# A one-core decoder step: the expert stage reordered, and the up projections made in split products

## The chip, the cores and the metric

The kernel runs on one core of a Trainium2 chip. The metric is the device time of one execution in microseconds (us); lower is better. Three runs of the kernel before gave 3391.62, 3391.7 and 3400.47 us, the median is 3391.7 us.

Engines are named as in the profile: PE multiplies matrices, PEld is its weight load, DVE is the vector engine, ACT the scalar engine, POOL GpSimd, SP the engine that only issues transfers. PSUM has eight banks, into which PE writes.

## What is computed

One layer is applied to T = 264 tokens: 256 of a prompt and 8 of a sample group. D is 2048.

```
proj  = rmsnorm(x) @ w_in                       # projections, attention, gated DeltaNet
x    += (sig(gA) * (o_fox @ w_up_fox) + sig(gB) * (o_gdn @ w_up_gdn)) @ w_out
h     = rmsnorm(x);  q = h @ w_q                # 8 heads, 2 x 128 keys each
s     = q . sub_keys;  two top-16 lists per head -> top-16 of 256 sums
idx, gate = ia * 128 + ib, softmax(top-16)      # 128 experts for each token
act   = gelu(h . u[idx]);  x += sum(act * gate * v[idx])     # 16384 experts
x    += sig(rmsnorm(x) @ w_ple_gate) * (p @ w_ple)
```

The kernel computes the expert part densely: for all 16384 experts it forms h . u, multiplies gelu of it by a weight that is zero where a token did not choose the expert, and multiplies by v.

## The kernel before

**Units.** All large weights pass through the core in units of 128 x 2048 f32 (1 MB), in the order of the list `STREAM`. SP loads a unit into one of four ring slots (`WR`). ACT copies each quarter of 512 columns to fp32r, the high part (`high_part`, L388); DVE subtracts it from the original to get the low part (`low_part`, L393). PE then makes three products for each 128 x 128 tile, high x high, high x low and low x high (`products`, L551 to L553): 48 matmuls of 264 columns for a unit. There is one buffer for the high and low parts of a quarter, so ACT may write a quarter only when PE is done with the same quarter of the unit before, and PE needs it three quarters later. Each engine follows an order written out by hand; `dense_steps` gives the usual one: four parts of the next unit, then the finishing work of this one.

**Up and out.** The two up projections (16 units) are plain f32 matmuls (L915) that read the ring slot directly. For each unit DVE multiplies the two results by their gates and adds (L1736 to L1740), ACT and DVE split the merged block into the parts that the out projection reads (L1200, L1742). `mt_ready` then releases the out projection (16 units, split products).

**Routing.** After the query projection `wq` PE multiplies queries and keys (`key_scores`, L942 and L934), and DVE finds the top-16 lists in three rounds, two of 128 tokens and one of the 8 sample tokens (`top16` and what follows, L1788 to L1851). `turn_results` turns each round's indices and gates over on PE.

**Gate weights, then experts, in two halves.** For 64 of the 128 first indices at a time, DVE makes one-hot rows (L1865, L1868), POOL multiplies them by the gates (L1335), PE multiplies the one-hots (L978) and ACT stores the dense gate weights of that half (L1231). Then come 128 units in groups: four units of u (scores, gelu L1249, weighing L1896 to L1900) and four of v (`outputs`, added to x by DVE at L1910). The loop body holds 16 units.

**After it** come the last norm and the per-layer embedding (16 units).

Of the kernel before, what the change touches and what calls it, by code (L numbers as in the profile page):

```python
# [15 lines left out]
ALU = mybir.AluOpType  # L16
# [23 lines left out]
HALF = N_KEYS // 2  # L40
PGW = NH * P
EG = 4

# [3 lines left out]
STREAM = [("A", 56), ("gates", 32), ("up", 16), ("out", 16), ("wq", 16), ("peer0", 128), ("peer1", 128), ("ple", 16)]  # L47
S0 = {}
_n = 0
for _name, _c in STREAM:  # L50
# [10 lines left out]
            ("norm1", 1), ("wq", 16), ("route", 12)]  # L61
for _h in range(2):
    JOB_LIST += [(f"wb{_h}", 66), (f"u{_h}", 64)]
JOB_LIST += [("norm2", 1), ("ple", 16)]
JOB = {}
SPLIT_JOBS = ("A", "gates0", "gates1", "out", "wq", "u0", "u1", "ple")
# [10 lines left out]
def split_index(s):  # L77

    return s if s < S0["up"] else s - 16


def stream_of(n):

    for name, s in (("A", S0["A"]), ("gates0", S0["gates"]), ("gates1", S0["gates"] + 16), ("out", S0["out"]),
                    ("wq", S0["wq"]), ("ple", S0["ple"])):
# [3 lines left out]
    for h in range(2):  # L89
        k = n - JOB[f"u{h}"]  # L90
        if 0 <= k < 64:
            return S0[f"peer{h}"] + (k if k < 4 else 4 + 8 * ((k - 4) // 4) + k % 4)
    return None
# [3 lines left out]
RS_JOBS = [[JOB["route"] + o for o in js] for js in ((0, 1, 2, 3), (4, 5, 6, 7), (9,))]  # L97
IDX_JOB = [JOB["route"] + o for o in (8, 10, 11)]
# [41 lines left out]
def build(nc, xT, pT, wd, vd, wsmall, wple, subk, kx, vx, lx, state, convst, params, consts, ptab,  # L140
          o_x, o_k, o_v, o_lf, o_sp, o_ss, o_cs):
    with ExitStack() as ctx:
# [37 lines left out]
        AL = AH + 2 * EG * T  # L180
        WSH, WSL = AH, AH + 384
        assert AL + 2 * EG * T <= NR
        sp_ = lambda a, n: split[:, a:a + n]
        as_f32 = lambda ap: ap.bitcast(F32)
        hh3 = sp_(HH, KT * T).rearrange("p (k t) -> p k t", t=T)
# [46 lines left out]
        WH = BIG  # L232
        AB = WH + HALF * T
        IDX = AB + 2 * T
        assert IDX + 3 * T <= BIG_END, IDX + 3 * T
        OHA = WR + 2 * D_MODEL
        OHB = OHA + 2 * 8 * HALF
        assert OHB + 2 * 8 * P <= WR + RING * D_MODEL

# [17 lines left out]
        assert SK >= HRAW + KT * T and SK + 16 * P <= IDX  # L257
        QZ = IDX + 3 * T
        assert QZ + 64 + NH * 136 <= BIG_END
# [33 lines left out]
        merged, mh_ready = sem("merged"), sem("mh_ready")  # L293
        ws_hi, ws_lo = sem("ws_hi"), sem("ws_lo")
        x_again = sem("x_again")
        aw_ready, ah_ready = sem("aw_ready"), sem("ah_ready")
# [36 lines left out]
        mg_step, oh_step = sem("merge_step"), sem("onehot_step")  # L333
# [16 lines left out]
        def bank(n):  # L350
            return ps[:, n % 4, :]

# [21 lines left out]
        def wait_slot(eng, it, m, s, back=0):  # L374

            if S0["up"] <= s < S0["out"]:
                eng.wait_ge(pe_job, it * m + (PJ[JOB["up"] + s - S0["up"]] - back))
            else:
                eng.wait_ge(lo_ready, it * (4 * m) + 4 * (split_index(s) + 1 - back))
# [49 lines left out]
        def _(sp):  # L429
# [70 lines left out]
            sp.wait_ge(mt_ready, 1)  # L500
# [3 lines left out]
            for half in range(2):  # L504
                s0, u0, v0 = S0[f"peer{half}"], 136 + 64 * half, 64 * half
                peel(s0, u0, PJ[JOB[f"wb{half}"] + 65])

                def group(it):

                    for kind in range(2):  # L510
                        for j in range(RING):
                            s = s0 + 4 + 4 * kind + j
                            wait_slot(sp, it, 8, s, RING)
                            load_w(it, 4, s, (wd, vd)[kind], ((u0 + 4) + j, v0 + j)[kind])

                with sp.Fori(0, 15) as it:
                    group(it)
                for j in range(RING):
                    wait_slot(sp, 0, 0, s0 + 120 + j)
                    load_w(0, 0, s0 + 124 + j, vd, v0 + 60 + j)  # L520
# [13 lines left out]
        def _(pe):  # L534
# [20 lines left out]
            def split_unit(it, m, s, n, mj=4, h0=None):  # L555


                if n >= 4 or not isinstance(it, int):
                    pe.wait_ge(evac[n % 4], it * (mj // 4) + n // 4)
                for q in range(RING):  # L560
                    wait_low_part(pe, it, m, s, q)
                    for kk in range(QK):
                        k = q * QK + kk
                        if h0 is not None:
                            pe.wait_ge(ht_ready, h0 + k + 1)
                        last = products(bank(n)[:, 0:T], ckh(q)[:, kk * P:(kk + 1) * P], ckl(q)[:, kk * P:(kk + 1) * P],
                                        hh3[:, k, :], hl3[:, k, :], k == 0, k == KT - 1)
                    last.then_inc(quarter_done, 1)

            def dense(name, its, h0=None):  # L570
                with pe.Fori(0, its) as it:
                    for j in range(RING):
                        split_unit(it, 4, S0[name] + j, JOB[name] + j, h0=None if j else h0)
# [333 lines left out]
            pe.wait_ge(of_ready, 1)  # L907
            with pe.Fori(0, 4) as it:
                for j in range(RING):
                    n = JOB["up"] + j  # L910
                    pe.wait_ge(w_loaded[j], it * 16 + 16 * (S0["up"] // 4 + 1))
                    pe.wait_ge(evac[n % 4], it + n // 4)
                    for half in range(2):
                        for k in range(NH):
                            last = mm(ps[:, n % 4 + 4 * half, 0:T], wr(j)[:, (half * NH + k) * P:(half * NH + k + 1) * P],  # L915
                                      ot3[:, half * NH + k, :], start=(k == 0), stop=(k == NH - 1))
                    last.then_inc(pe_job, 1)
            pe.wait_ge(mt_ready, 1)
            dense("out", 4)
# [6 lines left out]
            def key_scores(c):  # L926
                if c == 2:
                    n, = RS_JOBS[2]
                    claim(pe, n)
                    pe.wait_ge(qz_ready, 2)  # L930
                    for p_ in range(2):
                        for h in range(NH):
                            hp = 2 * h + p_
                            last = mm(bank(n)[0:64, p_ * P:(p_ + 1) * P], at(QZ + hp * 64, 64), at(SK + hp * P, P),  # L934
                                      start=(h == 0), stop=(h == NH - 1))
                    last.then_inc(pe_job, 1)
                    return
                for g, n in enumerate(RS_JOBS[c]):
                    claim(pe, n)
                    for i in range(4):  # L940
                        hp = 4 * g + i
                        last = mm(bank(n)[:, i * P:(i + 1) * P], at(QT + hp * T + c * P, P), at(SK + hp * P, P),  # L942
                                  start=True, stop=True)
                    last.then_inc(pe_job, 1)

            def turn_results(c):
                n = IDX_JOB[c]
                claim(pe, n)
                pe.wait_ge(res_ready, c + 1)
                for i in range(3):  # L950
                    if c == 2:
                        last = mm(bank(n)[:, i * P:i * P + NS], at(LX + i * P, P, 64), at(ROW_T, NS, 64), start=True, stop=True)
                    else:
                        last = nc.tensor.transpose(bank(n)[:, i * P:(i + 1) * P], at(RES + i * P, P), ident)  # L954
                last.then_inc(pe_job, 1)

            key_scores(0)
            key_scores(1)
            turn_results(0)
            key_scores(2)  # L960
            turn_results(1)
            turn_results(2)


            for half in range(2):
                wb, ub = JOB[f"wb{half}"], JOB[f"u{half}"]

                def weights_of(it, j):


                    pe.wait_ge(oha_ready, it * 4 + (33 * half + j + 1))
                    pe.wait_ge(ohb_ready, it * 4 + (33 * half + j + 1))
                    for n in (wb + 2 * j, wb + 2 * j + 1):
                        pe.wait_ge(evac[n % 4], it * 2 + n // 4)
                        for i in range(4):
                            t = 4 * (n - wb - 2 * j) + i
                            oha = at(OHA + (j % 2) * 8 * HALF + t * HALF, HALF)
                            last = mm(bank(n)[:, i * P:(i + 1) * P].rearrange("p (r a) -> p r a", a=HALF),  # L978
                                      at(OHB + (j % 2) * 8 * P + t * P, P),
                                      oha.unsqueeze(1).broadcast_to([P, 2, HALF]), start=True, stop=True)  # L980
                        last.then_inc(pe_job, 1)

                with pe.Fori(0, 8) as it:
                    for j in range(4):
                        weights_of(it, j)
                weights_of(8, 0)

                s0 = S0[f"peer{half}"]

                def scores(it, m, s, n):  # L990
                    for j in range(RING):
                        split_unit(it, m, s + j, n + j, m // 2)

                def outputs(it, m, s, g, buf):

                    for dq in range(RING):
                        for q in range(RING):
                            if dq == 0 and q == 0:
                                pe.wait_ge(a_blk, it * (m // 2) + (4 * (16 * half + g) + 4))

                            pe.wait_ge(y_added, it * (2 * m) + (16 * (16 * half + g) + 4 * dq + q + 1))
                            wait_low_part(pe, it, m, s + dq, q)
# [1023 lines left out]
```

## Time and profile before

| | us |
|---|---|
| median of three runs | 3391.7 |
| profiled execution, first to last instruction (its span) | 3393.9 |
| PE busy in it | 3112.1 |
| DVE busy | 1973.4 |
| ACT busy | 1291.3 |
| POOL busy | 190.1 |

The profile is one execution. Its span is the only time that it gives of itself. It lies 2.2 us above the median and within the three runs. PE's busy time counts overlapping matmuls once; groups of matmuls on different lines overlap each other, so their sums exceed the span.

### The profile page before, as it was taken

To read this page: it belongs to the slowest core of one execution; us is meant where nothing else is said; L and a number is where in the kernel's file an instruction comes from. 1 tells how busy PE (TensorE), PEld (TensorE's weight loads), DVE (VectorE), ACT (ScalarE), POOL (GpSimd) and SP (SyncE) were. 2 spreads that over 40 slices of the span, in tenths; PEclk is the share of its full clock that TensorE was granted. 3 is DMA by queue.
4 is the path that set the end of the run, shared out by engine and by line. 5 is a ranking of instruction groups with operands and counts; after the bars stand their busy time and mean duration, and the time that the engine had idled before them with its cause. 6 is when DMAs were issued, how large, how long until landed. Compare 5 with 4: busy or idle time off the path is not lost.

```text
span 3393.9 us, 63208 instructions
## 1 busy us (share of the span) xinstructions
PE 3112.1 (92%) x23603; PEld 2921.9 (86%) x23603; DVE 1973.4 (58%) x3888; ACT 1291.3 (38%) x2225; POOL 190.1 (6%) x203
## 2 busy tenths in 40 slices
PE   6999899799999998922899999999889999999989
PEld 6999689499755787922799999999889999999979
DVE  4477466422233235488766666666766666666654
ACT  4455320122222024411544444444444444444444
POOL 0000110000000000002400000000330000000000
PEclk8999899599999999966999999999999999999989
DMA  5555200356576444400155455455225554545543
GB/s 192 177 184 180 85 1 8 127 199 245 200 250 214 185 160 148 173 0 0 70 180 184 177 182 182 177 185 175 73 99 176 184 179 180 184 175 185 178 148 125
DMA packets 82022, 519.76 MB, mean 153 GB/s; under 512 B 9186, under 2 KB 9458, under 8 KB 28914
## 3 DMA queue, kind: packets, MB, share of 16 engines
q1 hardware_dynamic: 69394, 468.36, 38.8%
q0 software_dynamic: 11360, 45.61, 3.7%
q10 hardware_dynamic: 1152, 4.19, 0.3%
q8 instruction: 78, 1.28, 0.1%
q14 instruction: 38, 0.31, 0.0%
HBM read 508.74 MB, written 9.39 MB: 153 GB/s over the span
## 4 chain that ended last, share of the span: by engine, by line
PE 88%; DVE 7%; POOL 2%; SPq 2%; issue 1%; ACT 0%; DMA 0%; POOLq 0%; DVEq 0%; ACTq 0%
PE ps L551 23%; PE ps L552 23%; PE ps L553 22%; PE ps L915 3%; PE ps L858 3%; PE ps L869 3%; PE ps L978 2%; POOL arena L1335 2%; PE ps L732 1%; SPq L465 1%; PE ps L611 1%; DVE arena L1865 1%; PE ps L546 1%; PE ps L720 1%; PE ps L603 1%
## 5 line engine op out<-in xcount | busy, mean ns | idle before, releaser
L551 PE MATMUL ps<-split 128*128 128x264 f32 x6288 | 1798.0, 286 | 53.9 <-DVE split L393 53.9
L552 PE MATMUL ps<-split 128*128 128x264 f32 x6288 | 1789.7, 285 | 0.0
L553 PE MATMUL ps<-split 128*128 128x264 f32 x6288 | 1784.7, 284 | 0.0
L393 DVE TENSOR_TENSOR split<-arena,split 128x512 fp32r<-128x512 f32 x1568 | 1078.6, 691 | 956.9 <-ACT split L388 954.1
L388 ACT ACTIVATE split<-arena 128x512 fp32r<-128x512 f32 x1568 | 987.8, 632 | 1401.5 <-PE ps L553 1401.1
L551 PEld LDWEIGHTS ps<-split 128*128 128x128 f32 x6288 | 1187.9, 189 | 73.9 <-issue 36.2
L552 PEld LDWEIGHTS ps<-split 128*128 128x128 f32 x6288 | 1188.3, 189 | 0.8
L553 PEld LDWEIGHTS ps<-split 128*128 128x128 f32 x6288 | 1183.6, 188 | 0.3
L1910 DVE TENSOR_TENSOR arena<-arena,ps 128x264 f32<-128x264 f32 x512 | 216.4, 423 | 5.9 <-PE ps L553 5.9
L1335 POOL TENSOR_TENSOR arena<-arena 128x512 f32<-128x512 f32 x66 | 121.7, 1844 | 1264.6 <-DVE arena L1865 1264.6
L978 PE MATMUL ps<-arena 128*128 128x128 f32 x1056 | 140.3, 287 | 38.9 <-POOL arena L1335 38.8
L978 PEld LDWEIGHTS ps<-arena 128*128 128x128 f32 x1056 | 128.3, 197 | 50.9 <-POOL arena L1335 32.9
L1231 ACT ACTIVATE arena<-ps 128x256 f32 x132 | 84.3, 638 | 106.7 <-PE ps L978 106.7
L915 PE MATMUL ps<-arena 128*128 128x264 f32 x512 | 116.8, 390 | 0.7 <-DVE arena L1721 0.7
L858 PE MATMUL ps<-arena 128*64 128x128 f32 x1024 | 116.0, 272 | 0.0
L915 PEld LDWEIGHTS ps<-arena 128*128 128x128 f32 x512 | 98.4, 192 | 18.8 <-issue 0.8
L858 PEld LDWEIGHTS ps<-arena 128*64 128x64 f32 x1024 | 112.2, 136 | 2.3
L869 PE MATMUL ps<-arena 128*8 128x512 f32 x256 | 112.7, 592 | 0.0
L954 PE MATMUL ps<-arena 128*128 128x128 f32 x6 | 1.8, 434 | 101.8 <-ACT arena L1216 51.8
L869 PEld LDWEIGHTS ps<-arena 128*8 128x8 f32 x256 | 21.5, 89 | 78.6 <-issue 76.0
L954 PEld LDWEIGHTS ps<-arena 128*128 128x128 f32 x6 | 1.0, 213 | 102.2 <-ACT arena L1216 52.0
L1865 DVE TENSOR_TENSOR arena<-arena 128x512 f32<-128x512 f32 x66 | 57.7, 875 | 40.1 <-PE ps L978 40.1
(299 smaller groups left out, 1696.4 us busy)
## 6 DMA issues: line engine op xcount, KB each, us to landing
arena<-in_wd SPq DMA_DIRECT2D x280, 1024.0 KB, 4.8
arena<-in_vd SPq DMA_DIRECT2D x128, 1024.0 KB, 4.8
arena<-in_kx POOLq DMA_DIRECT2D x32, 512.0 KB, 6.4
arena<-in_kx SPq DMA_DIRECT2D x32, 512.0 KB, 4.5
arena<-in_vx SPq DMA_DIRECT2D x32, 512.0 KB, 4.3
arena<-in_vx POOLq DMA_DIRECT2D x32, 512.0 KB, 4.4
arena<-in_state POOLq DMA_DIRECT2D x8, 512.0 KB, 6.7
o_ss<-arena ACTq DMA_DIRECT2D x8, 512.0 KB, 7.5
```

The source lines that it names most:

```text
L388: nc.scalar.activation(ckh(q), at(WR + (s % 4) * D_MODEL + q * QW, QW), ACT.Copy).then_inc(hi_ready, 1)
L393: nc.vector.tensor_tensor(ckl(q), at(WR + (s % 4) * D_MODEL + q * QW, QW), as_f32(ckh(q)), ALU.subtract).then_inc(lo_ready, 1)
L551: mm(out, wh, xh, start=start, stop=False)
L552: mm(out, wh, xl, start=False, stop=False)
L553: return mm(out, wl, xh, start=False, stop=stop)
L858: last = mm(score[:, j, :], at(QM + (s * NH + h) * 64, 64), page(j)[:, h * P:(h + 1) * P], start=False, stop=False, skip_group_check=True)
L869: last = mm(ps[0:NS, b + i, :], at(PRT + j * 64 + s * NH, NH), page(j)[:, i * 512:(i + 1) * 512], start=(j == 0), stop=(j == PAGES - 1))
L915: last = mm(ps[:, n % 4 + 4 * half, 0:T], wr(j)[:, (half * NH + k) * P:(half * NH + k + 1) * P], ot3[:, half * NH + k, :], start=(k == 0), ...
L978: last = mm(bank(n)[:, i * P:(i + 1) * P].rearrange("p (r a) -> p r a", a=HALF), at(OHB + (j % 2) * 8 * P + t * P, P), oha.unsqueeze(1).br ...
L1335: nc.gpsimd.tensor_tensor(oh, oh, gate, ALU.mult).then_inc(oha_ready, 1)
L1865: V.tensor_tensor(oh, cst(C_IOTA + half * HALF, HALF).unsqueeze(1).broadcast_to([P, 8, HALF]), ia, ALU.is_equal).then_inc(oh_step, 1)
L1910: V.tensor_tensor(xt3[:, d, :], xt3[:, d, :], ps[:, 4 + q, 0:T], ALU.add).then_inc(y_added, 1)
```

## The change

**Order of the expert stage.** All 128 units of u come first, written out unit by unit on every engine, then all 128 units of v, in a loop whose body holds 8 units. One buffer of gelu results is no longer enough, so the scores of each pair of units are written to device memory (`scores_spill`) and read back by POOL, four units at a time.

**Routing beside the scores.** Only the first `key_scores` stands before the units. The second comes after unit 2, the turned results after units 19, 36 and 41. On DVE the operations of the top-16 lists and the low parts of the u units are woven together: `beside` counts estimated time of routing work and puts in one low part for every 0.8 us of it; `lows_until` forces the low parts up to a unit before DVE waits for PE or ACT. The expected places of ACT's exponentials and of the turned results are constants (`EXP_AT`, `TURN_AT`).

**Gate weights beside the scores.** They are built for 4 tokens a step, 66 steps, all 128 first indices at once. 33 steps follow units 43 to 64 and 33 follow units 95 to 116, one or two for a unit. The first half of the tokens is written to device memory (`gates_spill`) after units 67 to 89, the second half stays on chip.

**Weighing.** POOL multiplies scores by gate weights, eight operations of 132 columns for a group of four blocks. ACT makes the high part and DVE the low part, beside the v units.

**Up projections.** They become split units like the others: ACT and DVE split `ot` (the branch outputs) into the operand parts and each up unit into high and low parts. The merged blocks keep their place in the gates' buffer; ACT makes their high parts beside the up units, DVE the 16 low parts after the last merge, and the first out unit waits for these one by one (`ml_ready`).

```diff
-STREAM = [("A", 56), ("gates", 32), ("up", 16), ("out", 16), ("wq", 16), ("peer0", 128), ("peer1", 128), ("ple", 16)]
+STREAM = [("A", 56), ("gates", 32), ("up", 16), ("out", 16), ("wq", 16), ("u", 128), ("v", 128), ("ple", 16)]
+EXP_AT = (13, 30, 38)
+TURN_AT = (19, 36, 41)
+W_FROM = (43, 95)
+SPILL_AT = tuple(67 + 3 * i // 2 for i in range(N_KEYS // SPILL))
...
# PE, up and scores
-            pe.wait_ge(of_ready, 1)
+            pe.wait_ge(ol_ready, 5)
...
+                    for q in range(RING):
+                        wait_low_part(pe, it, 4, S0["up"] + j, q)
+                        for i in range(QK):
+                            k = q * QK + i
+                            last = products(ps[:, n % 4 + 4 * (k // NH), 0:T], ckh(q)[:, i * P:(i + 1) * P],
+                                            ckl(q)[:, i * P:(i + 1) * P], hh3[:, k, :], hl3[:, k, :], k % NH == 0, k % NH == NH - 1)
+                        last.then_inc(quarter_done, 1)
...
+            for k in range(N_KEYS):
+                split_unit(0, 4, S0["u"] + k, JOB["u"] + k)
+                if k == KEYS1:
+                    key_scores(1)
+                for c in range(3):
+                    if k == TURN_AT[c]:
+                        turn_results(c)
+                if k == TURN_AT[0]:
+                    key_scores(2)
+                for g in w_steps_after(k):
+                    build_weights(g)
...
+            with pe.Fori(0, GROUPS // 2) as it:
+                for b in range(2):
+                    outputs(it, 2 * EG, S0["v"] + EG * b, b)
...
# SP
+            for k in range(N_KEYS):
+                wait_slot(sp, 0, 0, S0["u"] + k - RING)
+                load_w(0, 0, S0["u"] + k, wd, 136 + k)
+                if k >= 6 and k % 2 == 0:
+                    write_scores(k - 6)
...
# ACT, in each u unit
+                if k >= 4 and k % 2 == 0:
+                    act.wait_ge(g_saved[(k // 2) % 2], 16 * (k // 4))
+                n = JOB["u"] + k
+                A(at(GST + (k % 4) * T, T), bank(n)[:, 0:T], ACT.Gelu).then_inc(evac[n % 4], 1)
...
# POOL
+            for g in range(GROUPS):
+                pool.wait_ge(gw_in[g % 2], 32 * (g // 2 + 1))
+                for j in range(EG):
+                    nc.gpsimd.tensor_tensor(score(g, j)[:, 0:TH], score(g, j)[:, 0:TH], weight(g, j), ALU.mult).then_inc(am_ready, 1)
+                    nc.gpsimd.tensor_tensor(score(g, j)[:, TH:T], score(g, j)[:, TH:T], kept(g, j), ALU.mult).then_inc(am_ready, 1)
+                if g == 0:
+                    for b in range(2):
+                        pool.wait_ge(g_saved[b], 16 * (N_KEYS // 4))
+                if g:
+                    pool.wait_ge(a_blk, EG * g)
+                if g + 1 < GROUPS:
+                    load_group(g + 1)
...
# DVE
+            def beside(us):
+
+                spent[0] += us
+                while spent[0] >= 0.8:
+                    spent[0] -= 0.8
+                    lows_until(lows[0] + 1)
...
+            def make_rows(g):
+
+                if g >= 2:
+                    dve.wait_ge(route_pe, ROUTE_JOBS + g - 1)
+                V.tensor_tensor(at(OHB + (g % 2) * WT * P, WT * P).rearrange("p (t b) -> p t b", b=P),
+                                cst(C_IOTA).unsqueeze(1).broadcast_to([P, WT, P]),
+                                at(IDX + T + WT * g, WT).unsqueeze(2).broadcast_to([P, WT, P]), ALU.is_equal).then_inc(ohb_made, 1)
+                for t in range(WT):
+                    n = WT * g + t
+                    ins = V.tensor_scalar(gate_rows(g, t), cst(C_IOTA), at(IDX + n, 1), at(IDX + 2 * T + n, 1), ALU.is_equal, ALU.mult)
+                ins.then_inc(rows_made, 1)
+
+            def rest_weighed(it, m, g, j):
+
+                dve.wait_ge(ah_ready, it * m + (EG * g + j + 1))
+                V.tensor_tensor(a_low(g, j), score(g, j), as_f32(a_high(g, j)), ALU.subtract).then_inc(a_blk, 1)
...
+            def add_outputs(it, m, s, g, last=False):
+
+                for dq in range(RING):
+                    for q in range(RING):
+                        if not (last and dq == RING - 1):
+                            low_part(dve, it, m, s + dq + 1, q)
+                        wait_quarter(dve, it, m, s + dq, q)
+                        d = 4 * dq + q
+                        V.tensor_tensor(xt3[:, d, :], xt3[:, d, :], ps[:, 4 + q, 0:T], ALU.add).then_inc(y_added, 1)
+                    if not last:
+                        rest_weighed(it, m, g + 1, dq)
```

## Rows read from the trace of the kernel before

**Rows 1.** Windows: start:end, length, busy PE, PEld, DVE, ACT, POOL, clock, DMA.
```profile
1453.95:1582.76 128.81, 15.21 (x109) 14.04 (x108) 117.85 (x509) 7.34 (x14) 0.00 (x0) 0.57 0.00 0
1582.76:1673.33 90.57, 70.19 (x528) 64.20 (x528) 66.29 (x66) 42.68 (x68) 61.29 (x33) 0.95 0.01 2
1673.33:2418.97 745.64, 744.76 (x6144) 744.58 (x6144) 507.06 (x959) 341.57 (x576) 0.00 (x0) 1.00 0.51 180
2418.97:2509.75 90.78, 70.15 (x528) 64.07 (x528) 66.53 (x67) 42.69 (x68) 60.38 (x33) 0.96 0.01 1
...
1119.72:1236.56 116.84, 116.81 (x512) 98.37 (x512) 24.55 (x60) 6.34 (x15) 0.48 (x1) 0.98 0.42 153
1236.56:1334.73 98.17, 94.58 (x768) 94.37 (x768) 50.74 (x83) 40.53 (x65) 0.00 (x0) 0.98 0.54 193
```

**Rows 2.** What PE waited for in 1673 to 3255: total, times, longest.
```profile
PE ps L978 <- POOL arena L1335: 19.4, 31, 3.2
PE ps L551 <- DVE split L393: 4.1, 2, 2.1
```

**Rows 3.** Chain that ended last, in order of time: start, length, work.
```profile
703.23 7.18 PE ps L858 x64
716.41 7.18 PE ps L858 x64
...
1595.13 2.07 PE ps L978 x16
```

**Rows 4.** Groups by line and shape: busy, mean ns, idle before.
```profile
L942 PE MATMUL ps<-arena 128*128 128x128 f32 x64 | 7.4, 275 | 0.5 <-issue 0.5
...
L1822 DVE TENSOR_TENSOR arena<-arena 128x2048 f32<-128x2048 f32 x4 | 9.0, 2284 | 0.0
...
L1305 POOL TENSOR_SCALAR arena<-arena 128x128 f32<-128x128 f32 x16 | 5.7, 371 | 20.8 <-PE ps L675 14.8 <-PE ps L690 6.0
```

**Rows 5.** Windows over the first two rounds of lists, columns as in rows 1.
```profile
1459.06:1513.00 53.94, 2.80 (x26) 2.61 (x24) 53.28 (x229) 1.49 (x3) 0.00 (x0) 0.56 0.00 0
1515.18:1569.00 53.82, 3.99 (x30) 3.75 (x29) 53.26 (x229) 0.31 (x1) 0.00 (x0) 0.56 0.00 0
```

**Rows 6.** Timeline of DVE in the v units: start, length, operation, idle before.
```profile
3237.02 0.69 DVE L393 TENSOR_TENSOR split<-arena,split 128x512 fp32r<-128x512 f32 x1 [0.43 <-ACT split L388]
3237.63 0.42 DVE L1910 TENSOR_TENSOR arena<-arena,ps 128x264 f32<-128x264 f32 x1
```

**Rows 7.** Timeline from the last up unit to the first out unit.
```profile
1238.62 2.19 ACT L388 ACTIVATE split<-arena 128x512 fp32r<-128x512 f32 x4
...
1239.36 2.50 DVE L393 TENSOR_TENSOR split<-arena,split 128x512 fp32r<-128x512 f32 x4 [0.21 <-ACT split L388]
...
1240.11 0.59 PE L551 MATMUL ps<-split 128*128 128x264 f32 x1 [3.58 <-DVE split L393]
```

**Rows 8.** Timeline from the last page of v to the first up unit.
```profile
1107.72 7.05 PE L869 MATMUL ps<-arena 128*8 128x512 f32 x16
...
1114.80 1.21 DVE L1712 TENSOR_TENSOR arena<-ps,arena 8x1024 f32<-8x1024 f32 x1 [18.59 <-PE ps L869]
...
1119.72 3.88 PE L915 MATMUL ps<-arena 128*128 128x264 f32 x8 [0.67 <-DVE arena L1721]
```

**Rows 9.** DMA issues: transfer, queue, count, size, median us to landing.
```profile
o_ss<-arena ACTq DMA_DIRECT2D x8, 512.0 KB, 7.5
...
arena<-in_kx POOLq DMA_DIRECT2D x32, 512.0 KB, 6.4
```

**Rows 10.** Timeline of DVE beside POOL where the gate weights are built.
```profile
1583.37 1.22 DVE L1868 TENSOR_TENSOR arena<-arena 128x1024 f32<-128x1024 f32 x1
1583.67 1.82 POOL L1335 TENSOR_TENSOR arena<-arena 128x512 f32<-128x512 f32 x1 [463.47 <-DVE arena L1865]
1584.50 1.53 DVE L1865 TENSOR_TENSOR arena<-arena 128x512 f32<-128x512 f32 x1
...
1589.44 0.69 DVE L1865 TENSOR_TENSOR arena<-arena 128x512 f32<-128x512 f32 x1 [2.27 <-PE ps L978]
```

More of the change, by code:

```diff
@@ L910, in _ @@
                     n = JOB["up"] + j
-                    pe.wait_ge(w_loaded[j], it * 16 + 16 * (S0["up"] // 4 + 1))
                     pe.wait_ge(evac[n % 4], it + n // 4)
[L913 to L919, printed above, removed]
+                    for q in range(RING):
[5 more added lines that the diff above has]
+                        last.then_inc(quarter_done, 1)
+            dense("out", 4, xh3=mh3, rest=ml_ready)
             norm(1)
@@ L959, in _ @@
[L959 to L1002, printed above, removed]
-                            for j in range(EG):
-                                a = (buf * EG + j) * T
-                                last = products(ps[:, 4 + q, 0:T], ckh(q)[:, j * P:(j + 1) * P],
-                                                ckl(q)[:, j * P:(j + 1) * P], sp_(AH + a, T), sp_(AL + a, T),
-                                                j == 0, j == EG - 1)
-                            last.then_inc(quarter_done, 1)
-                scores(0, 0, s0, ub)
-                with pe.Fori(0, 7) as i2:
-                    for b in range(2):
-                        scores(i2, 16, s0 + 4 + 8 * b, ub + 4 + 4 * b)
-                        outputs(i2, 16, s0 + 8 + 8 * b, b, b)
-                scores(0, 0, s0 + 116, ub + 60)
-                outputs(0, 0, s0 + 120, 14, 0)
-                outputs(0, 0, s0 + 124, 15, 1)
@@ new lines, in _, with merged_high @@
+            for q in range(RING):
+                high_part(act, 0, 0, S0["up"], q)
+            act.wait_ge(of_ready, 1)
+            act.wait_ge(oh_ready, 4)
+            A(hh3[:, 0:NH, SEQ:T], ot3[:, 0:NH, SEQ:T], ACT.Copy).then_inc(oh_ready, 1)
+            def merged_high(it, j):
+                act.wait_ge(merged, it * 4 + (j + 1))
+                m = arena[:, bass.ds(it * (4 * T) + (GT + j * T), T)]
+                A(split[:, bass.ds(it * (4 * T) + (MH + j * T), T)], m, ACT.Copy).then_inc(mh_ready, 1)
@@ new lines, in values @@
+            def values(it, m, s, g, last=False):
+                for j in range(EG):
+                    for q in range(RING):
+                        if not (last and j == EG - 1):
+                            high_part(act, it, m, s + j + 1, q)
+                    if not last:
+                        split_weighed(it, m, g + 1, j)
+            with act.Fori(0, GROUPS // 2 - 1) as it:
+                for b in range(2):
+                    values(it, 2 * EG, S0["v"] + EG * b, b)
+            values(0, 0, S0["v"] + EG * (GROUPS - 2), GROUPS - 2)
@@ L1747, in add_to_x @@
+            dense_steps(dve, S0["up"], 4, low_part, merge, False, False)
+            for k in range(KT):
+                if k == 0:
+                    dve.wait_ge(mh_ready, KT - 1)
+                if k == KT - 1:
+                    dve.wait_ge(mh_ready, KT)
+                V.tensor_tensor(hl3[:, k, :], blk(GT, k), as_f32(mh3[:, k, :]), ALU.subtract).then_inc(ml_ready, 1)
             def add_to_x(it, j):
@@ L1754, in _ @@
             dve.wait_ge(x_again, 16)
-            dense_steps(dve, S0["out"], 4, low_part, add_to_x)
+            dense_steps(dve, S0["out"], 4, low_part, add_to_x, first=False)
             for j in range(RING):
@@ L1923, in _ @@
+            with dve.Fori(0, GROUPS // 2 - 1) as it:
+                for b in range(2):
+                    add_outputs(it, 2 * EG, S0["v"] + EG * b, b)
+            add_outputs(0, 0, S0["v"] + EG * (GROUPS - 2), GROUPS - 2)
+            add_outputs(0, 0, S0["v"] + EG * (GROUPS - 1), GROUPS - 1, True)
+            dve.wait_ge(y_added, 4 + GROUPS * KT)
             dve.sem_inc(x2_ready, 1)
```

448 lines of the change are left out of this document (236 added, 212 removed).

## The prediction, made before the changed kernel ran

> **What bounds the kernel now.** I read the stage windows first [rows 1]. In the unit stages PE is the bound: in the first half of the expert stage it is busy for 744.8 of 745.6 us at the full clock of 2.4 GHz (1.00), while DVE works 507 and ACT 342. That is 745.6 / 128 = 5.83 us for a unit, 1.46 us for a quarter. PE's waits inside the two halves come to 4.1 us on the low parts of the weights [rows 2]. So nothing but fewer matmuls shortens a unit, and a unit is free for other engines as long as the low parts come in time. What remains are the stretches in which PE waits. The reader is to see three: routing takes 128.8 us with PE busy for 15.2 and DVE for 117.9, at a clock of 0.57, and the gate weights take 90.6 and 90.8 us with no unit running. The other place is the up stage, 116.8 us, where PE is busy but on plain f32 passes.
>
> **The expert stage: what is removed.** The three stretches vanish from PE's path: 128.8 + 90.6 + 90.8 = 310.2 us. What comes back, on PE unless said:
>
> Key scores and turned results are the same matmuls, so PE's busy time of the routing window returns, 15.2 us, with the 0.5 us wait ahead of it [rows 1, 4]: 15.7.
>
> Gate weights: 66 steps of 4 matmuls, each two passes in f32, 528 passes; before it was 1056, since each half handled all tokens. A pass costs 0.112 us with 64 weight columns (7.18 / 64) and 0.129 in the old weights (2.07 / 16) [rows 3]; the same shape in the key scores costs 7.4 / 64 = 0.115 [rows 4]. I take 0.115: 60.7 us (59.1 to 68.1).
>
> Changing over from unit to other matmuls and back: in the gate stage, whose units are also written out one by one, one unit with 64 page passes takes 716.41 - 703.23 = 13.18 us [rows 3]. Less 7.18 and 5.83, that leaves 0.17. There are 44 units with weight steps and four with routing work: 48 x 0.17 = 8.2 us (0 if it is hidden, 11.9 at one for each of 70 insertions). This row also answers for the unrolled code: 17 instructions a us were issued there without a gap, as many as a unit now needs (96 in 5.83 us).
>
> Routing on DVE costs nothing where it fits between low parts. A low part holds DVE for 0.61 us (3237.02 to 3237.63 [rows 6]), four for a unit are 2.4 of 5.83. The estimates in `beside` sum to 46.3 us for a full round (lists 18.0 + 12.9, sums 2.6, selection 11.8, 1.0), so 57 low parts are woven in, 14.25 units. DVE then needs 53.9 [rows 5] + 57 x 0.61 = 88.7 us, PE 14.25 x 5.83 + 3.7 for the second key scores = 86.8. The second round: 53.8 + 58 x 0.61 = 89.2 against 84.5 + some 5.6 of turned results and third key scores. The two are level. A low part may be late by three quarters less ACT's copy and its own time, 4.37 - 0.6 - 0.7 = 3 us, before PE notices. Single selection operations of 2.28 us [rows 4] use up most of that slack, several times. I take 3 us of stalls; ends: 0, and 11 if low parts occupy their full 0.69. After unit 43 DVE has the one-hot rows instead, one and a half steps a unit at 0.69 for 512 columns [rows 10] and four of 128 columns at 0.25, an estimate between a quarter of that and its half: 5.0 with the low parts, in units that PE then makes 5.83 + 1.5 x 0.92 long. Covered; if it were not, each us over would be paid 44 times.
>
> The waits. ACT's exponentials and PE's turned results stand in their queues behind units whose low parts DVE has already been forced to issue (`lows_until`), so what the high parts queue behind is ready. Gelu of a unit waits for a score write issued some 16 us earlier (the ring has four blocks); the longest landing of a write row is 7.5 us [rows 9]. SP's score writes stand ahead of weight loads, but their gelu is done when the slot before them comes free. All this I cost at nothing. If the writes took 1 us more than the ring allows, every second unit would pay it, 64 us.
>
> u to v: the first v quarter needs the last score weighed, which stands on DVE behind the fourth low part of v. High part and low part of the last quarter (1.3 us), the subtraction 0.43: PE stops for 2.0 us (1 to 3.6, the stop before the out stage [rows 7]). Group 1 then needs the buffer of the last scores: gelu and write (3 to 7 us), POOL's load (6.4 [rows 9]), a multiplication, its high part, a low part behind it: 13 to 18 us after the last u unit. PE wants it at 2.0 + 2 x 5.83 = 13.7. I take 1.5 us, once (0 to 5). Later groups have 23.3 us for a load and eight multiplications.
>
> The v loop has the products, low parts and additions of before. Sum: 15.7 + 60.7 + 8.2 + 3 + 2 + 1.5 = 91.1 back, so the stage gains 219.1.
>
> **POOL beside DVE** is the one cost that the trace makes me weigh. Where the gate weights were built, DVE's L1865 takes 0.69 us alone, but 1.53 when it starts beside POOL's multiplication: POOL ends at 1585.49, DVE at 1586.03 [rows 10]. It stood still until POOL was done. POOL's 1.82 in turn begins under DVE's L1868, which ends at 1584.59; 0.90 remain for 512 columns. The new multiplications have 132 columns; bounds are 0.37 for 128 columns with one tile read [rows 4] and 1.82 [rows 10]. I take 0.4, nearest in size. Eight are 3.2 us of standing still for a group. DVE's idle in 16 quarters is 16 x 0.43 [rows 6] = 6.9 us, less four new subtractions of 0.35 (0.42 for 264 columns, less the 0.08 by which operations overlap): 5.5. Hidden. The Trainium skill, "SBUF — State Buffer", section "Who interferes with whom", states it as a lock: a DVE instruction with two SBUF inputs and a GpSimd instruction that reads SBUF exclude each other for the whole instruction. The trace agrees (1.53 against 0.69 us). By it the low parts wait and the additions, which read PSUM, do not; by the rows alone, with 3.2 against 5.5, the sum is the same.
>
> **Up and out.** Removed 116.8. The units now cost 16 x 5.83 = 93.2. Their start is late: after the last gate unit (1107.7) ACT makes four copies of 1024 columns, 1.1 each by its 2.19 for four of 512 [rows 7], and DVE four subtractions of some 1.2 and four low parts (2.5), in order, before L1712. That ends about 1116.5, where L1712 began at 1114.80 [rows 8]: 1.7 late, and 0.7 for the split of the last columns. The clock of 0.98 in 116.8 us [rows 1] means 4.7 us at 1.2 GHz, which costs 2.3; it stays. The stop before the out stage was 3.58 us [rows 7]; now it is high and low part (1.4), three merge steps (1.2), one low part and a signal (0.7): 3.3. The other 15 low parts take 0.35 each, PE's three products 0.364 (5.83 / 16). Sum: -116.8 + 93.2 + 1.7 + 0.7 + 2.3 - 0.3 = -19.2 (-23 to -15).
>
> **Together**: 3393.9 - 219.1 - 19.2 = 3155.6 for the span. The median lay 2.2 us under the span, so 3153.
>
> **The rivals.**
>
> *DVE sets the pace of units 0 to 42.* For: 88.7 against 86.8, before any waiting. Against: 3 us of slack, and the rounds end with low parts alone. If each of 172 low parts cost PE 0.15 us: 26 us in place of the 3, 3176.
>
> *POOL's lock outgrows DVE's idle time in the v loop.* At 0.9 us a multiplication it is 7.2 - 5.5 = 1.7 us a group, 32 groups: 54 us, 3207. For: L1865's 1.53. Against: the sum above. The rule that makes it possible is the one named above (the Trainium skill, "SBUF — State Buffer", section "Who interferes with whom").
>
> *The same, slower than before.* At 1.82 us it is 14.6 - 5.5 = 9.1 a group: 291 us, 3444. It decides at 5.5 + 238 / 32 = 12.9 us a group, 1.6 us a multiplication. For: the row's 1.82. Against: half of that was waiting, for four times the columns.
>
> *Routing isn't hidden.* If the waits in the weave left PE standing while DVE works the lists, up to 117.9 us come back: 3271. Against: DVE's list work waits for PE nowhere but at the turned results.
>
> **How the numbers follow.** Forecast 0.66, its own range 3137 (no change-over, no stalls) to 3183 (upper ends of the passes, of DVE and of both hand-overs together). DVE's pace 0.13, POOL's lock at 0.9 0.09, slower 0.03, routing exposed 0.05; 0.04 for what I don't see, half of it near no change. The range is 3137 to 3200: it takes in DVE's pace and leaves out the rest. A change under 0.3% (10 us) can't be told from none. Faster 0.95, same 0.02, slower 0.03.
>
> **What would show it.** PE without stops of over 10 us from the last query unit to the last v unit; 5.83 us a unit in both halves, 7.3 in units 43 to 64 and 95 to 116; up near 96 us; POOL's multiplications at 0.4 us and low parts beside them at 0.7 to 1.1. I am wrong if PE's waits on L393's successor exceed 20 us, if a v group takes over 23.5 us, or if ACT waits for score writes.

## The result and the profile after

The changed kernel took 3272.5 us in the median (3272.3 to 3278.6) against 3393.2 for the kernel before on the same chip: a ratio of 0.9639, 95% interval 0.9622 to 0.9656. It is faster, but by 121 us where 238 were forecast (219.1 + 19.2); 3272 lies far above the range of 3137 to 3200. The profiled span is 3277.0 us (before 3393.9). One execution of the last experiment took 7611.3 us where its other three took 3142.7 to 3148.9; it is left out of every comparison.

The 116.9 us between the two spans lie as follows, to 0.1 us, by the starts in the chains of the two traces. Up and out gain 22.7 (216.9 to 194.2 us) and lose 2.0 by a later start; the stretch from the second norm to the key scores loses 1.6, the stages ahead of up lose 4.7, in which nothing was changed. The expert stage gains 102.6 (1802.0 to 1699.4), where 219.1 were forecast. Of the miss, 116.5 us lie in that stage. Its windows answer to [rows 1] (columns as there): three of the u units, one of the v loop, and, last, the up stage.

```profile
1443.99:1716.00 272.01, 266.60 (x2176) 264.39 (x2176) 228.67 (x690) 133.81 (x233) 0.00 (x0) 0.99 0.55 190
1716.00:1875.00 159.00, 159.00 (x1339) 159.00 (x1338) 111.98 (x248) 97.26 (x145) 0.00 (x0) 1.00 0.47 161
...
2047.00:2260.00 213.00, 213.00 (x1787) 213.00 (x1786) 139.02 (x289) 124.58 (x195) 5.88 (x10) 1.00 0.52 181
2300.00:2600.00 300.00, 274.70 (x2106) 272.45 (x2105) 200.20 (x395) 124.59 (x220) 68.66 (x110) 0.94 0.51 184
...
1126.46:1223.00 96.54, 94.66 (x768) 94.45 (x768) 59.95 (x111) 43.68 (x79) 0.00 (x0) 0.98 0.51 186
```

The u units are what the prediction wanted: PE stands for 5.4 of 272 us while routing runs beside the units, and not at all from 1716 to 2260. The v loop, which was thought to be untouched, is not: in 300 us PE stands for 25 and its clock is 0.94. It makes 2106 matmuls there; at the pace of [rows 1] (6144 in 745.64) it would make 2472. What PE waits for, answering to [rows 2]:

```profile
PE ps L606 <- DVE split L1985: 73.5, 32, 2.4
PE ps L606 <- DVE split L441: 51.6, 10, 15.6
...
PE ps L606 <- DVE split L1821: 3.1, 1, 3.1
```

The second row lies almost all in earlier stages (5.3 us of it in the u units), the third is the stop before the out stage (3.3 forecast). The first is new: 32 stops, one for each group of v, for L1985. That is the subtraction in `rest_weighed`. The timeline shows why, first three rows of POOL and DVE for later use, then the end of group 1 (columns as in [rows 6]):

```profile
2290.61 0.92 POOL L1395 TENSOR_TENSOR arena<-arena 128x132 f32<-128x132 f32 x1
...
2291.49 0.47 POOL L1396 TENSOR_TENSOR arena<-arena 128x132 f32<-128x132 f32 x1
...
2291.68 0.82 DVE L441 TENSOR_TENSOR split<-arena,split 128x512 fp32r<-128x512 f32 x1
...
2318.64 0.63 ACT L436 ACTIVATE split<-arena 128x512 fp32r<-128x512 f32 x1 [0.83 <-PE ps L608]
2319.17 0.41 ACT L1279 ACTIVATE split<-arena 128x264 fp32r<-128x264 f32 x1
2319.30 0.69 DVE L441 TENSOR_TENSOR split<-arena,split 128x512 fp32r<-128x512 f32 x1 [0.43 <-ACT split L436]
2319.91 0.42 DVE L2004 TENSOR_TENSOR arena<-arena,ps 128x264 f32<-128x264 f32 x1
...
2320.25 0.43 DVE L1985 TENSOR_TENSOR split<-arena,split 128x264 fp32r<-128x264 f32 x1
...
2320.90 0.39 PE L606 MATMUL ps<-split 128*128 128x264 f32 x1 [2.30 <-DVE split L1985]
2321.13 0.30 PE L607 MATMUL ps<-split 128*128 128x264 f32 x1
2321.25 0.40 PE L608 MATMUL ps<-split 128*128 128x264 f32 x1
```

PE finishes the group's last quarter at 2318.60. That frees the place for the last high part on ACT (2318.64), and behind it stand, in program order, DVE's low part of it (2319.30), the addition of the quarter just finished (L2004), and only then the subtraction of the next group's fourth score block (L1985). PE's first quarter of the next group waits for that one (`a_blk`). ACT's copy of the block (L1279) was done at 2319.58, POOL's product long before. So two queues make up the stop of 2.3 us: ACT's high part and copy, which end 0.98 us after PE does, and DVE's low part and addition, which put the subtraction off until 2320.25.

The rest of the v loop's loss is the clock. Behind such a stop PE's passes follow each other at 0.22 us in place of 0.12 (2321.45 and 2321.67 are the next two starts). Over the v loop from 2284 to 3130 PE was busy for 774.4 us with 5942 matmuls; the run without these stops (below) has 5979 in 726.0, which makes 721.5 for 5942. So 53 us are clock and 71.6 are stops.

The chain in the u units, answering to [rows 3]: a gate-weight step has 8 passes, two steps in one unit and one in the next.

```profile
1717.65 1.78 PE ps L1022 x16
1725.23 0.89 PE ps L1022 x8
1731.92 1.78 PE ps L1022 x16
```

A pass costs 1.78 / 16 = 0.111 us. Two units with their 24 passes take 14.27 us: 2.67 for the passes, 5.80 for a unit. That is no more than the 5.83 of a unit in [rows 1], so these rows leave nothing for changing over between them.

### The profile page after: what moved, and what is told of

It reads as the page before. It is cut to its first block, busy times and chain, and to the rows that moved or that the text cites. A ratio compares the mean times of both kernels' runs of the same rounds, so it can differ in the third digit from the quotient of the medians.

```text
span 3277.0 us, 60857 instructions
## 1 busy us (share of the span) xinstructions
PE 3068.8 (94%) x23331; PEld 2899.6 (88%) x23331; DVE 1905.2 (58%) x3899; ACT 1363.1 (42%) x2361; POOL 269.7 (8%) x457
## 4 chain that ended last, share of the span: by engine, by line
PE 87%; DVE 7%; SPq 2%; issue 1%; ACT 1%; DMA 1%; POOL 0%; DVEq 0%; ACTq 0%; POOLq 0%
PE ps L606 24%; PE ps L607 24%; PE ps L608 23%; PE ps L916 4%; PE ps L927 3%; PE ps L1022 2%; DVE split L441 2%; PE ps L790 2%; SPq L513 1%; PE ps L669 1%; PE ps L601 1%; PE ps L778 1%; PE ps L661 1%; ACT split L436 1%; SPq L514 1%
## 5 line engine op out<-in xcount | busy, mean ns | idle before, releaser
L606 PE MATMUL ps<-split 128*128 128x264 f32 x6544 | 1903.2, 291 | 129.8 <-DVE split L1985 73.5
L607 PE MATMUL ps<-split 128*128 128x264 f32 x6544 | 1883.4, 288 | 0.0
L608 PE MATMUL ps<-split 128*128 128x264 f32 x6544 | 1876.7, 287 | 0.0
L441 DVE TENSOR_TENSOR split<-arena,split 128x512 fp32r<-128x512 f32 x1632 | 1134.3, 701 | 1062.1 <-ACT split L436 1051.5
L606 PEld LDWEIGHTS ps<-split 128*128 128x128 f32 x6544 | 1259.1, 192 | 157.9 <-DVE split L441 118.9
L607 PEld LDWEIGHTS ps<-split 128*128 128x128 f32 x6544 | 1260.6, 193 | 0.8
L608 PEld LDWEIGHTS ps<-split 128*128 128x128 f32 x6544 | 1253.9, 192 | 0.3
L2004 DVE TENSOR_TENSOR arena<-arena,ps 128x264 f32<-128x264 f32 x512 | 215.9, 422 | 3.0 <-PE ps L608 3.0
L1395 POOL TENSOR_TENSOR arena<-arena 128x132 f32<-128x132 f32 x128 | 89.1, 696 | 169.9 <-DMA arena<-gates_spill 169.9
L1396 POOL TENSOR_TENSOR arena<-arena 128x132 f32<-128x132 f32 x128 | 84.9, 663 | 0.0
L1979 DVE TENSOR_SCALAR arena<-arena 128x128 f32<-128x128 f32 x264 | 73.6, 344 | 0.0
L1274 ACT ACTIVATE arena<-ps 128x512 f32<-128x512 f32 x66 | 69.8, 1130 | 0.0
L1022 PE MATMUL ps<-arena 128*128 128x128 f32 x528 | 66.1, 274 | 0.0
L1022 PEld LDWEIGHTS ps<-arena 128*128 128x128 f32 x528 | 62.7, 191 | 0.0
L1102 ACT ACTIVATE arena<-ps 128x264 f32 (+1 forms) x120 | 45.0, 375 | 40.0 <-PE ps L608 39.9
L1985 DVE TENSOR_TENSOR split<-arena,split 128x264 fp32r<-128x264 f32 x128 | 54.7, 427 | 2.3 <-ACT split L1279 2.3
```

Source lines behind the costliest of these rows:

```text
L441: nc.vector.tensor_tensor(ckl(q), at(WR + (s % 4) * D_MODEL + q * QW, QW), as_f32(ckh(q)), ALU.subtract).then_inc(lo_ready, 1)
L606: mm(out, wh, xh, start=start, stop=False)
L607: mm(out, wh, xl, start=False, stop=False)
L608: return mm(out, wl, xh, start=False, stop=stop)
L1022: last = mm(bank2(n)[:, t * P:(t + 1) * P], at(OHB + ((g % 2) * WT + t) * P, P), gate_rows(g, t), start=True, stop=True)
L1395: nc.gpsimd.tensor_tensor(score(g, j)[:, 0:TH], score(g, j)[:, 0:TH], weight(g, j), ALU.mult).then_inc(am_ready, 1)
```

## The experiments

**The fourth block's weighing moved ahead.** In ACT's loop and in DVE's the fourth block is handled behind the second quarter of the group's last unit; the other three stay behind the fourth quarter of theirs.

```diff
-                    if not last:
-                        rest_weighed(it, m, g + 1, dq)
+                        if not last and q == (1 if dq == EG - 1 else RING - 1):
+                            rest_weighed(it, m, g + 1, dq)
```

> The changed kernel with one edit: in each v group, ACT's high part and DVE's subtraction for the last block of the next group stand behind the second quarter of the fourth unit, not behind its last. Theory (stop and clock): PE stops 2.3 us at the head of each of 32 groups, because the last subtraction stands behind the last addition, and runs at the lower clock after it; both go, 73.5 + some 53 us, so 3146 to 3155 us and a clock of 1.00 in the v units. Rival (POOL's lock): DVE is late because of POOL's multiplications and the stop only shows it; then at most a few us a group come back, above 3230. Rival (the clock falls by itself): only the stops go, 3199.

Measured: 3154.5 us (3146.9 to 3155.0), ratio 0.9272 [0.9249, 0.9295]: 118 us below the changed kernel, by one `if` on each engine. PE's waits for L1985 fall from 73.5 to 2.0 us, which is the one at the first v group. Its v loop:

```profile
2300.00:2600.00 300.00, 300.00 (x2471) 300.00 (x2470) 237.53 (x464) 146.18 (x257) 81.02 (x130) 1.00 0.61 215
```

PE stands nowhere, at the full clock, with POOL's multiplications and the low parts as before. So the place of the fourth block's weighing, at the end of ACT's and DVE's orders, is the cause of the miss. The edit moves both the copy and the subtraction; the next one parts them.

**A shorter stop.** Only DVE's subtraction moves, to just ahead of the group's last low part; ACT's copy stays where it was.

```diff
+                        if not last and dq == EG - 1 and q == RING - 1:
+                            rest_weighed(it, m, g + 1, dq)
                         if not (last and dq == RING - 1):
                             low_part(dve, it, m, s + dq + 1, q)
...
-                    if not last:
+                    if not last and dq < EG - 1:
```

> The changed kernel with one edit: only DVE's subtraction for the last block moves, ahead of the group's last low part and addition; ACT's high part of that block stays behind the last quarter. The stop should shrink from 2.3 to about 1.5 us and not vanish. Theory (stop and clock): if the clock still falls after a stop of 1.5 us, 3272 - 31 x 0.8 = 3247; if it no longer falls, 3195. Rival (POOL's lock): no change, 3272.

Measured: 3208.4 us (3204.4 to 3211.3), ratio 0.9435 [0.9413, 0.9457]. There are still 32 stops, of 1.7 us (54.0 in all). DVE now stands and waits for ACT's copy (a row from the end of a group), so the subtraction's place on DVE alone is not the whole cause. But the clock does not fall:

```profile
2288.74 0.43 DVE L1985 TENSOR_TENSOR split<-arena,split 128x264 fp32r<-128x264 f32 x1 [0.73 <-ACT split L1279]
...
2300.00:2600.00 300.00, 279.89 (x2280) 277.44 (x2279) 217.75 (x428) 135.01 (x238) 72.21 (x117) 1.00 0.55 199
```

Of the 54 us above the run before, 52 are the stops (54.0 less the 2.0 that stayed there). Against the changed kernel it gains 64 us, only 19.5 of them shorter stops.

**Between the two.** The subtraction behind the last low part, ahead of the last addition.

```diff
                             low_part(dve, it, m, s + dq + 1, q)
+                        if not last and dq == EG - 1 and q == RING - 1:
+                            rest_weighed(it, m, g + 1, dq)
                         wait_quarter(dve, it, m, s + dq, q)
```

> The changed kernel with DVE's subtraction of the next group's fourth block put behind the group's last low part but ahead of its last addition (in the changed kernel it is behind the addition). The stop loses the addition's 0.42 us: 2.3 - 0.4 = 1.9 us in 32 groups, PE waits about 60 us on it. If a stop of 1.9 us leaves the clock at 2.4 GHz as one of 1.7 us does, the time is 3154.5 + 60 = 3215; if the clock falls as it does behind stops of 2.3 us, some 45 us more: 3260.

Measured: 3257.2 us (3251.7 to 3260.1), ratio 0.9584 [0.9567, 0.9601]. PE waits 63.0 us in 32 stops, 2.0 us each, and the clock falls:

```profile
2300.00:2600.00 300.00, 278.34 (x2168) 276.09 (x2167) 209.31 (x407) 128.36 (x226) 73.49 (x118) 0.95 0.51 187
```

PE stands for 21.7 of 300 us here and for 20.1 in the run ahead of this one, nearly the same, but the matmuls fall from 2280 to 2168. In this loop stops of 1.7 us leave the clock at 2.4 GHz (1.00), stops of 2.0 don't (0.95). Of the 103 us above 3154.5, 61 are stops and some 42 are clock.

**POOL's work doubled.** Of the rivals that would take the time out of the range, the one with the highest chance (0.09) was that POOL's multiplications hold DVE up. The first experiment's kernel does each of them twice, the second time into unused space.

```diff
+                    for i, other in enumerate((weight(g, j), kept(g, j))):
+                        nc.gpsimd.tensor_tensor(cst(C_INV + (2 * j + i) * TH, TH), score(g, j)[:, i * TH:(i + 1) * TH], other, ALU.mult).then_inc(twice, 1)
```

> The kernel of the run with the last block early, and POOL does each of its multiplications a second time into unused space (the result isn't read): 16 of 132 columns for a group. Theory (stop and clock): POOL's multiplications are hidden in DVE's idle 5.5 us a group and partly wait themselves; the time stays within 10 us of the run with the last block early. Rival (POOL's lock): 16 x 0.68 us = 10.9 us of lock for a group against 5.5 us of idle, (10.9 - 5.5) x 32 = 172 us more, about 3320.

Measured: 3156.2 us (3148.0 to 3156.6), ratio 0.9276 [0.9253, 0.9300], no different from 3154.5.

```profile
2300.00:2600.00 300.00, 300.00 (x2472) 300.00 (x2471) 243.86 (x465) 146.18 (x259) 154.77 (x242) 1.00 0.61 215
```

POOL is busy for 155 us in place of 81, and PE still never stands. The lock itself is there: in the timeline above a low part of 0.69 us takes 0.82 beside POOL, and POOL's 0.47 becomes 0.92. But DVE's busy time grows by only 6.3 us in the 300 (237.5 to 243.9), and its idle time takes that. The rival is refuted.

**Fewer low parts beside routing.** DVE issues a low part for every 1.0 us of estimated list work instead of 0.8.

```diff
-                while spent[0] >= 0.8:
-                    spent[0] -= 0.8
+                while spent[0] >= 1.0:
+                    spent[0] -= 1.0
```

> The changed kernel with fewer low parts per unit of routing work on DVE: one for each 1.0 us of estimated list work in place of 0.8. If DVE and PE are level in units 0 to 42, as the prediction had it, a unit's four low parts now wait behind 4 x 0.2 = 0.8 us more of lists; over the 14 units of each of two weavings that is 11 us each: PE waits 15 to 25 us for low parts in the u stage, and the time is 3288 to 3298 in place of 3272. If DVE has slack that the trace of before did not show, PE's waits for low parts in the u stage stay under 8 us and the time stays within 4 us of 3272.

Measured: 3286.0 us (3282.5 to 3291.0), ratio 0.9669 [0.9652, 0.9686], 13.5 us above the changed kernel. PE's waits for low parts in the u units, the changed kernel's first and then this one's:

```profile
PE ps L606 <- DVE split L441: 5.3, 6, 3.0
```

```profile
PE ps L606 <- DVE split L441: 13.0, 19, 2.3
```

They grow by 7.7 us, and the first subtraction L1985 starts 13.1 us later (2.2 of which were there at the key scores already). The waits, 13.0 us in all, are less than the 15 to 25 expected of a DVE without slack and more than the 8 of one with plenty. I read it as DVE and PE nearly level in these units, with a little slack on DVE. At 0.8 the rival "DVE sets the pace" did not come about, but it was near.

**The up projection alone**, in the kernel before, whose expert stage stays as it was.

> The kernel before with the change to the up projection alone (split products, the merge in DVE's place between the low parts, merged columns split for the out stage); the expert stage is that of before. If the two parts of the change don't touch each other, the saving is the one read from the two profiles, up start to the end of out: 216.9 - 194.2 = 22.7 us, less 2.0 for the later start, some 20 us: 3372 against 3393, a ratio near 0.994. Rival: part of these 20 us came from the stages ahead of it (another clock at the hand-over from the gates); then under 12 us are left.

Measured: 3411.9 us (3408.9 to 3418.9) against 3395.0, ratio 1.0045 [1.0031, 1.0060]: slower by 17 us where 20 were to be gained. Up and out themselves do gain (194.3 us from the first up product to the norm, as in the changed kernel). The loss is in the second half of the expert stage, which the edit doesn't touch. Waits of PE, and a few of its pieces in the chain:

```profile
PE ps L551 <- issue: 15.8, 6, 2.7
...
PE ps L553 <- issue: 8.2, 6, 1.8
```

```profile
2614.10 1.08 issue
...
2619.25 1.57 issue
...
2713.16 1.30 issue
...
2719.22 0.59 issue
```

PE waits for nothing that the profile shows but its next instruction, twice in each of six turns of the loop of 16 units (99 us apart). In that half, 2500 to 3250, the instruction queue moved 64 packets; in the kernel before 13 (queue, packets, MB, share):

```profile
q8 instruction: 64, 1.05, 0.5%
```

```profile
q8 instruction: 13, 0.21, 0.1%
```

That is 51 packets more in some seven turns. I read it so: the loop's code, held over all its turns in the kernel before, is here fetched again in each. The price in that window (columns as in [rows 1]):

```profile
2500.00:3250.00 750.00, 725.98 (x5875) 723.19 (x5874) 484.86 (x916) 327.21 (x554) 0.00 (x0) 0.98 0.49 174
```

24 us of stops, and 13 of clock (5875 matmuls take 713 at the pace of [rows 1]): 37 lost. Is it the edit's doing, or only that the longer up stage ahead of the loop moved its code? Three kernels get 128 more PE instructions, waits for a semaphore reached long ago, where PE stands for the second norm anyway:

```diff
             norm(1)
+            for _ in range(128):
+                pe.wait_ge(ws_lo, 1)
```

The up projection alone, moved:

> The kernel of the run with the up projection alone, with 128 more PE instructions (waits for a semaphore that has long been reached) where PE waits for the second norm's sums anyway; nothing else differs. In that run the up stage gained what it should, but in the second half of the expert stage the instruction queue moved 64 packets in place of 13, and PE stopped for its next instruction twice in each turn of the unit loop. Theory: whether the loop's code stays on the chip hangs on where it lies in the program, and the more PE rows ahead of it moved it. Then 128 more can end the stops (some 3375, 13 packets in each half) or leave them, or bring them to the first half. Rival: the stops come from the up projection's other doings (weights, splits); then nothing changes: 3412, 64 packets in the second half and 13 in the first. A result without stops refutes the rival; one with the same stops tells little.

Measured: 3420.3 us, ratio 1.0061 [1.0044, 1.0077], no faster, but the stops have changed places. They now lie in the first half, with 64 packets there, and the second half has 11:

```profile
1780.45 1.33 issue
...
1785.65 1.75 issue
...
1879.73 1.29 issue
```

The kernel before, moved:

> The kernel before with the same 128 more PE instructions at the same place, and no other edit. If the place of the loop's code decides alone, a kernel that computes exactly what it did may now stop for its code in one of the halves: some 37 us longer for one half (what the run with the up projection alone lost in its second half), 3430. If the place does not matter: 3393 to 3397 and 13 packets in each half.

Measured: 3394.9 us, ratio 0.9994 [0.9983, 1.0005]; 13 packets in the second half, 12 in the first, no stops.

The first of them refutes that the new up stage's computing makes the stops: waits that compute nothing took them out of one half and put them into the other. So it matters where the loop's code lies. That this alone decides isn't shown, and which places are bad the runs don't tell: with the new up stage one of the two halves was hit each time, in the kernel before neither half at either place.

**All four weighings moved**: in each group to quarters of units 2 and 3 (and for group 0 to u units 120 to 123), so that the change from u to v has no stop either.

```diff
+WEIGH_AT = {(2, 0): 0, (2, 2): 1, (3, 0): 2, (3, 1): 3}
...
-                    if not last:
-                        rest_weighed(it, m, g + 1, dq)
+                        if not last and (dq, q) in WEIGH_AT:
+                            rest_weighed(it, m, g + 1, WEIGH_AT[dq, q])
```

> The changed kernel with all weighing for the next group in the third and fourth unit of a group, done by the second quarter of the fourth, and the first group weighed beside u units 120 to 123. Theory: the stops at the heads of the groups go as in the run with the last block early; the stop between u and v (2 us) and the wait for the scores of the second group (some 3 us), with the lower clock behind them, go too: 5 to 9 us below that run, about 3142. Rival: that wait is set by the write and load of the last scores and stays; then it equals the run with the last block early.

Measured: 3149.6 us (3139.8 to 3150.7), ratio 0.9255 [0.9231, 0.9280], 5 us below the first experiment, which is within the spread of the runs of either; but PE no longer waits for this subtraction anywhere, 2.0 us less. The same kernel with the 128 waits:

> The fastest version so far (the changed kernel with all four weighings of a group moved to quarters with slack) with the same 128 more PE instructions at the same place. Its unit code before the v loop is passed once, and its v loop has 8 units in place of 16. If half the loop's size is what keeps its code on the chip wherever it lies: 3150 within 5 us, under 12 packets on the instruction queue in the v loop, no stops for code. If a loop of 8 units can be moved out of place as one of 16 can: stops of 2 to 3 us in each of 16 turns, 40 us and more: 3190.

Measured: 3144.6 us, ratio 0.9245 [0.9227, 0.9264], 7 packets in 2510 to 3250 and no stops for code. In the two places tried, the loop of 8 units has no such stops.

## Why the prediction was wrong

The step that failed is "The v loop has the products, low parts and additions of before." The prediction did see the four new subtractions of a group, and costed them as time on DVE: four of 0.35 us against idle time, hidden. As time they are hidden: with the last one moved, PE stands nowhere, though all four are still there. But the weighing of the last block, ACT's copy and DVE's subtraction, was last in both queues at the moment when PE had nothing else, and its cost is not its length but the length of the queues ahead of it. The prediction had followed exactly this wait at one place, "u to v", and priced it right, at 2.0 us. It did not see that the same wait comes at the end of every group. 32 stops of 2.3 us are 73.5 us, and the fall of the clock behind them, which it had not considered there, is 53 more in the profile. Its own mark for being wrong, a v group of over 23.5 us, is met: the starts at 2293.41 and 2320.90 are 27.5 us apart.

The rival "Routing isn't hidden" gives 3271, within 2 us of the measured time. That is chance: PE stands for 5.4 us beside routing, not 117.9.

With that step mended by one edit the kernel takes 3154.5 against the forecast of 3153. That is closer than the terms were, and partly luck: the u units came out 9 us shorter than forecast, the stages ahead of the expert stage in which nothing was changed 6.3 us longer. The ends of the prediction's own range, 3137 and 3183, do not follow from the terms named for them, which give some 3142 and 3174. The terms:

- The three stretches gone from PE's path (310.2 us): right. No stop of over 3 us is left between the key scores and the last v unit.
- The u units: some 829 us forecast from 1443.99 on (745.6 for units, 60.7 + 8.2 + 3, and the 11.4 of 15.7 that lie behind the first key scores), measured 819.5 to PE's stop at 2263.5. Passes were 0.111 for 0.115 (2 us), changing over 0 for 8.2 us, stalls 5.3 for 3. The 0.17 us taken from the gate stage did not carry over; PE waits for nothing there either (690 to 900), and why it changes over without cost here is not shown.
- Waits for score writes, the turned results and the exponentials, costed at nothing: right, PE stands 0 of 544 us from 1716 to 2260, and before that only for low parts.
- The change from u to v: 2.0 forecast, 2.0 measured; group 1: 1.5 forecast, 0.2 measured. The load it waited for landed in 7.96 us and DVE stood until 2277.08, but PE went on until 2278.90.
- POOL's multiplications: 0.4 us forecast, 0.70 and 0.66 in the mean of L1395 and L1396, since about half of them stand still for a low part; 0.46 to 0.47 without. This waiting is more than forecast and cost PE nothing. The Trainium skill ("SBUF — State Buffer", section "Who interferes with whom") names both directions of the lock; the rows agree, 0.92 for 0.47 and 0.82 for 0.69.
- Up and out: 19.2 forecast. Counted from the end of the last page of v (1114.77 in [rows 8], 1119.50 here) the start came 2.0 us later (1.7 + 0.7 forecast); the up stage takes 96.5 us (near 96 forecast), the stop behind it 3.1; 22.7 - 2.0 = 20.7 in all. Right in the changed kernel. Put alone into the kernel before, the same edit makes it slower, through stops for another loop's code, of which the trace of before shows no sign.

## What to carry to other kernels

Cost a new instruction twice: once as time on its engine, and once by its place, asking what stands ahead of it in the queue, and in the queue that feeds it, when the engine that needs it runs dry. A wait that is priced at a hand-over should be looked for at every other place that runs the same lines; multiply before calling it small. And test the parts of a change apart with care: a part can lose alone what it gains in company, perhaps only through code that it moves.

## What the runs showed of the hardware

- PE's clock after short, regular stops: with 32 stops of 1.7 us, one in each group, the granted clock in the v loop is 1.00; with stops of 2.0 us it is 0.95, with 2.3 us 0.94, the passes behind a stop following at 0.22 us in place of 0.12. The fall costs 42 and 53 us on top of the 61 and 72 of the stops.
- A loop's code: for all turns of a loop of 16 units 11 to 13 packets of 16 KB were fetched in six of eight cases, 64 in the other two, with two stops in a turn, of up to 2.9 us. The Trainium skill ("Runtime: NRT & Kernel Launch", section "Instruction fetch mechanics") says that a taken branch to a page that is not held forces a fetch and stalls. The stops of these two cases agree with it. That the same loop runs without them in the other six, it does not explain, and the measurement decides.
